# A two-layer streaming encoder step: another order in the attention rounds, a 128-row own block, and tile-by-tile normalisation in the first combine

## The chip, the cores and the metric

The kernel runs on one core of a Trainium2 chip. The metric is the device time of one execution in microseconds (us), as the median of several. The engines named below are TensorE (PE, matrix products), VectorE (DVE), ScalarE (ACT), GpSimd (POOL) and SyncE (SP, which here only issues DMA). They run side by side and meet at semaphores.

## The reference

Two layers run on two groups of tokens with the same weights: 528 prompt tokens (16 learned meta tokens and 512 new ones) and 64 sample tokens, with caches of 512 past tokens for the latter. All is float32, of width 1024.

```
for layer in (0, 1):
    y = even_mixer(x) if layer == 0 else odd_mixer(x)
    x = layer_norm(ALPHA * x + y)
    x = layer_norm(ALPHA * x + moe(x))     # 16 experts, best group of 4, then top 2 in it
```

- The even mixer (layer 0) has four heads of a gated linear recurrence and four heads of forgetting attention ("fox"): softmax(q.k * scale + F_t - F_s) over earlier keys, times v.
- The odd mixer (layer 1) is multi-head latent attention ("MLA") with eight heads: keys and values are made from a 256-wide latent and a rotated 64-wide key shared by the heads. A token sees its own chunk of 64 and all before.
- For a token, the mixture adds the rows of its two experts, each with its weight, to the residual; then comes the normalisation.

## The kernel before, in words

**Tokens and tiles.** The 592 tokens lie in five tiles: tiles 0 to 3 with 128 prompt tokens each, tile 4 with the 64 sample tokens and the 16 meta tokens. The kernel's code is one list of instructions per engine, each in the order of its Python function (`block.tensor`, `block.vector`, `block.scalar`, `block.gpsimd`, `block.sync`). An engine runs its list in order and waits where it says so. PSUM is held as four pairs of banks. Each use of a pair is a ticket; `claim` (PE) waits until the user before it on the pair is released, and `filled` (the reader) waits for PE.

**Attention rounds.** Attention is a list of units, `att_units`. In the fox attention a unit is one head and one tile: four heads of five, 20 units. In MLA the units stand in two groups of four heads; a head has four units for tiles 0 to 3. The sample tokens are computed in the latent space ("absorbed"): one "pair" unit for two heads at a time (128 query rows, 64 own keys and 512 past keys, two sets of value products of 128 latent columns each), after the first and the second head of each group, four in all. One "meta" unit serves the meta tokens of all heads.

A unit goes through these steps, with the line that the profile shows:

- scores: PE multiplies queries with keys (L1330) and adds the mask by a bf16 product with an identity (L1335), in pair 0 or 1 in turn;
- max: VectorE takes the row maximum. In fox it adds the forget sums on the way (L2180) and then negates (L2183); in MLA it is one reduction (L2185);
- exp: ScalarE (L1852 fox, L1859 MLA), with the row sums;
- scale: VectorE inverts the sum (L2191) and scales the row (L2192);
- transposes: PE transposes the own block (L1347) and each block of 128 earlier keys (L1349) into pair 2 or 3 in turn. This claims the pair from the unit two before;
- VectorE copies the own block (L2200), ScalarE the others (L1869);
- values: PE multiplies the own block's values (L1372) and then the others' (L1374) into the same pair;
- output: VectorE copies the result to where the output projection reads it (L2212), which releases the pair.

Rounds interleave the units. In round n, PE does scores of n, values of n-3 and transposes of n-2. VectorE does max of n, output of n-3, own block of n-2 and scale of n-1. ScalarE does exp of n and its copy of n-2. The last unit of a stretch is followed by rounds without scores, the drain. Fox rounds run from 308.8 to 361 us of the span, the MLA groups from 772 to 830 and from 864 to 923.

**The own block.** `own_keys` says which columns of the probabilities are a unit's own keys and at which partitions they land once transposed. For an ordinary unit they are 128 rows, for a pair unit 64 (L1372's weights are then 64 x 128, taken from `cvo`, the latents of tile 4), for the meta unit 16.

**The first combine.** After the experts of layer 0, GpSimd gathers for each token its two experts' rows (L1017). VectorE does for each tile `combine_tile` (L2512, L2514: residual plus two weighted rows), `combined_stats` (L2523 to L2525 statistics, L2529 centring and gain) and `combined_norm` (L2539: scale and offset, into `rb`). Between the last two GpSimd computes the inverse root of the variance in two small operations (L883 adds epsilon, L884 is the power). `combine_tile(1)` stands ahead of `combined_norm(0)`, and so on by one tile. PE waits for the first operation of tile 0's combine, runs 24 products whose result nobody reads (`keep_busy`, L1447), waits for the normalised tile, transposes it (L1105) and begins the next layer's input projection (L1614) as soon as ScalarE has copied the transposes (L1708). The transposes of tile i+1 stand in the midst of tile i's projection.

Of the kernel before, what the change touches and what calls it, by code (L numbers as in the profile page):

```python
# [23 lines left out]
SEQ, NS, NM, PAST = 512, 64, 16, 512  # L24
# [7 lines left out]
QL, KVL, NOPE, ROPE = 512, 256, 128, 64  # L32
# [114 lines left out]
def build_step(nc, const_where, consts, a, o):  # L147
# [11 lines left out]
    with ctx:  # L159
# [116 lines left out]
        cvo = cvb[:, 0, :]  # L276
# [11 lines left out]
        kpst = r2.take(4 * 128).rearrange("p (j n) -> p j n", j=4)  # L288
        qrd = r3.take(4 * 128).rearrange("p (k s) -> p k s", k=4)
        qrm = r3.take(MH * NM)  # L290
        assert max(r2.n, r3.n) <= ARENA - ATT

        rtmp = arena[:, ARENA - 1024:ARENA].rearrange("p (b n) -> p b n", b=4)
# [436 lines left out]
        def own_keys(n):  # L730

            kind, _, i = att_units[n]
            if kind == "pair":
                return slice(NM, 80), slice(0, NS)
            if kind == "meta":
                return slice(NS, 80), slice(NS, 80)
            R = TILES[4] if i == 4 else 128
            return slice(0, R), slice(0, R)
# [360 lines left out]
        def _(pe):  # L1099
# [253 lines left out]
            def att_values(n):  # L1353
# [7 lines left out]
                if kind == "fox":  # L1361
                    hc = slice(128 * h, 128 * h + 128)
                    values = [(fv[rows, 4, hc], [(vp if i == 4 else fv)[:, j, hc] for j in range(nb)])]
                elif kind == "mla":
                    hc = slice(128 * (h % 4), 128 * (h % 4) + 128)
                    values = [(mv_[rows, 4, hc], [mv_[:, j, hc] for j in range(nb)])]
                else:
                    outs.append(psum[pair_of[("PT", n)]][:, 384:512])
                    values = [(cvo[rows, 128 * c:128 * c + 128], [ckpv[:, j, 128 * c:128 * c + 128] for j in range(nb)])
                              for c in range(2)]  # L1370
                for out, (vo, vb) in zip(outs, values):
                    last = pe.matmul(out, vo, pT[rows, n % 2, 512:512 + P], start=True, stop=(nb == 0))  # L1372
# [4 lines left out]
            def attention(first, last):  # L1377
                for n in range(first, last + 3):
                    if n < last:
                        att_scores(n)  # L1380
                    if n - 3 >= first:
                        att_values(n - 3)
                    if first <= n - 2 < last:
                        att_transpose(n - 2)

            pe.wait_ge(*lf_sb["x"])
            pe.wait_ge(*fq_sb[3])
# [56 lines left out]
            def keep_busy(n):  # L1444

                for _ in range(n):
                    pe.matmul(psum[1][:, 0:512], identb[:, :], const("m_past"), start=True, stop=True)  # L1447
# [153 lines left out]
                pe.transpose(ps[:, 768:768 + P], kpb[0:P, i % 2, :], ident[0:P, 0:P]).then_inc(pe_full.sem(("mt", i)), 1)  # L1601

            pe.wait_ge(*cb_sb[(0, "first")])
            keep_busy(24)
            pe.wait_ge(*r_sb[(1, 0)])
            transpose_tile(1, 0, rb[:, 0, :])
            for i in range(NT):
# [407 lines left out]
        def _(dve):  # L2015
# [198 lines left out]
            def attention(first, last):  # L2214
                for n in range(first, last + 3):
                    if n < last:
                        att_max(n)
                    if n - 3 >= first:
                        att_out(n - 3)
                    if first <= n - 2 < last:  # L2220
                        att_own(n - 2)
                    if first <= n - 1 < last:
                        att_scale(n - 1)

            def pad_probs():


                for buf in probs[1:]:
                    dve.memset(buf[:, 0:64], 0.0)
                dve.memset(probs[0][:, 0:64], 0.0).then_inc(pz_sb.sem, 1)  # L2230
# [312 lines left out]
            dve.memset(peT[0:64, 1, :], 0.0).then_inc(pez_sb.sem, 1)  # L2543
            combine_tile(0)
            combined_stats(0)
            combine_tile(1)
            combined_norm(0)
            combined_stats(1)
            combine_tile(2)
            combined_norm(1)  # L2550
            combined_stats(2)
            for i in range(NT):
                if i + 3 < NT:
# [25 lines left out]
            dve.wait_ge(*pe_full[("pt", 3)])  # L2579
            dve.memset(qrd, 0.0)  # L2580
            dve.memset(qrm, 0.0).then_inc(pez_sb.sem, 1)
            pad_probs()
            for g in range(2):
                key = ("qa", g)
# [99 lines left out]
```

## Time and profile before

| what | value |
|---|---|
| median of 3 runs | 1240.25 us (1239.88 to 1240.64) |
| profiled execution, its own time | 1235.15 us |
| its span | 1233.1 us |
| PE busy | 1119.4 us (91%) |
| VectorE busy | 559.4 us (45%) |
| ScalarE busy | 254.0 us (21%) |
| GpSimd busy | 222.4 us (18%) |
| mean granted TensorE clock | 0.97 |

Busy time is the sum of an engine's instructions over the span. Neighbouring products of PE overlap in their records, and their ends are modelled, so the distance between two starts is the better measure of what a product takes. Times in rows count from the start of the span. A bracket at the end of a row gives how long the engine had been idle, and what ended that.

### The profile page before, as it was taken

The numbers are of one execution on the slowest core, as the hardware profiler recorded it, in microseconds if no ns is written. First come the engines' busy times: TensorE is split into PE (matmuls) and PEld (weight loads), VectorE is DVE, ScalarE is ACT, GpSimd is POOL, SyncE is SP. The second block draws the span as 40 slices with busy tenths as digits, with TensorE's granted clock in tenths as the row PEclk, the third lists the DMA queues.
The fourth block names the chain that finished last, engine by engine and source line by source line (L and its number), as shares of the span: only waits on it lengthen the run. The fifth ranks groups of instructions, "written<-read, shape, count | busy, mean of one in ns | idle before, by whom it ended". The sixth has DMA issues, their size and how long they took to land.

```text
span 1233.1 us, 18806 instructions
## 1 busy us (share of the span) xinstructions
PE 1119.4 (91%) x7327; PEld 623.0 (51%) x7332; DVE 559.4 (45%) x1346; ACT 254.0 (21%) x610; POOL 222.4 (18%) x382
## 2 busy tenths in 40 slices
PE   8999999999889979999949989999999988999965
PEld 4556777554664633333315546776774553333312
DVE  2079879610643353744357140440442354554336
ACT  1214245321420000111101122332320000111112
POOL 0106445420201110101044210000000111100114
PEclk9999999999899989999989999999999989999987
DMA  8103302261734186999766222001205175899835
GB/s 355 69 9 141 125 33 105 86 226 65 44 130 175 52 345 246 339 413 375 281 214 222 70 106 69 1 1 68 69 8 231 62 298 209 329 397 407 316 103 196
DMA packets 41974, 215.54 MB, mean 175 GB/s; under 512 B 4504, under 2 KB 6104, under 8 KB 32544
## 3 DMA queue, kind: packets, MB, share of 16 engines
q1 hardware_dynamic: 24432, 153.28, 31.8%
q0 software_dynamic: 17168, 60.27, 15.8%
q8 instruction: 59, 0.97, 0.3%
q10 hardware_dynamic: 288, 0.80, 0.2%
q14 instruction: 27, 0.22, 0.1%
HBM read 181.02 MB, written 33.29 MB: 174 GB/s over the span
## 4 chain that ended last, share of the span: by engine, by line
PE 78%; DVE 9%; issue 4%; DMA 3%; ACT 3%; POOL 1%; DVEq 0%; SPq 0%; ACTq 0%
PE pair L1516 12%; PE pair L1131 9%; PE pair L1410 9%; PE pair L1537 7%; PE pair L1252 5%; PE pair L1330 5%; PE pair L1614 5%; PE pair L1142 4%; PE pair L1374 3%; PE pair L1119 2%; PE pair L1502 2%; PE pair L1372 2%; DMA ring<-in_even_w_in 2%; DMA arena<-x_rows,ints 1%; PE pair L1647 1%
## 5 line engine op out<-in xcount | busy, mean ns | idle before, releaser
L1516 PE MATMUL pair<-ring,arena 128*32 128x512 f32 x608 | 128.5, 595 | 0.0
L1131 PE MATMUL pair<-ring,xT 128*128 128x512 f32 x256 | 111.3, 593 | 0.9 <-DMA ring<-in_even_w_in 0.9
L1516 PE MATMUL pair<-arena 128*32 128x512 f32 x736 | 100.5, 600 | 8.0 <-issue 4.5
L1252 PE MATMUL pair<-xT,ring 128*128 128x296 f32 x320 | 85.1, 421 | 6.9 <-ACT arena L1726 3.0
L883 POOL TENSOR_SCALAR small<-small 128x1 f32<-128x1 f32 (+3 forms) x45 | 15.2, 337 | 386.9 <-DVE small L2264 334.5
L905 POOL TENSOR_TENSOR arena<-arena 128x128 f32<-128x128 f32 x140 | 58.4, 451 | 145.5 <-PE pair L1178 78.9
L1131 PEld LDWEIGHTS pair<-ring,xT 128*128 128x128 f32 x256 | 48.1, 190 | 59.7 <-issue 57.9
L1330 PE MATMUL pair<-arena 128*128 128x264 f32 (+8 forms) x270 | 74.6, 407 | 2.8 <-ACT arena L1716 1.8
L1031 POOL DMA_INDIRECT arena<-x_rows,ints x26 | 26.4, 1014 | 264.9 <-PE pair L1502 163.4
L1252 PEld LDWEIGHTS pair<-xT,ring 128*128 128x128 f32 x320 | 60.4, 193 | 25.8 <-issue 9.3
L2402 DVE COPY arena<-pair 128x256 f32<-128x256 f32 x26 | 11.0, 423 | 135.4 <-PE pair L1525 135.4
L1537 PE MATMUL pair<-ring,arena 128*32 128x512 f32 x304 | 67.5, 611 | 4.0 <-DVE arena L2402 4.0
L1516 PEld LDWEIGHTS pair<-ring,arena 128*32 128x32 f32 x608 | 33.7, 110 | 57.6 <-issue 57.6
L1516 PEld LDWEIGHTS pair<-arena 128*32 128x32 f32 x736 | 30.4, 111 | 63.4 <-issue 63.4
L1614 PE MATMUL pair<-ring,xT 128*128 128x512 f32 (+3 forms) x160 | 57.3, 513 | 1.1 <-ACT xT L1708 1.1
L1410 PE MATMUL pair<-ring,mixT 128*128 128x512 f32 x128 | 57.7, 593 | 0.5 <-issue 0.5
L1410 PE MATMUL pair<-ring,xT 128*128 128x512 f32 x128 | 57.5, 592 | 0.0
L1516 PE MATMUL pair<-xT,arena 128*32 128x512 f32 x320 | 56.3, 592 | 0.0
L1708 ACT COPY xT<-pair 128x1024 f32<-128x1024 f32 (+1 forms) x15 | 14.2, 949 | 189.3 <-PE pair L1105 189.3
L1537 PE MATMUL pair<-arena 128*32 128x512 f32 x368 | 53.1, 608 | 0.0
L1330 PEld LDWEIGHTS pair<-arena 128*128 128x128 f32 (+1 forms) x270 | 43.6, 192 | 12.7 <-issue 5.9
L1374 PE MATMUL pair<-arena 128*128 128x128 f32 (+1 forms) x336 | 48.4, 278 | 0.0
(385 smaller groups left out, 1968.1 us busy)
## 6 DMA issues: line engine op xcount, KB each, us to landing
arena<-in_moe_w_gate_up SPq DMA_DIRECT2D x14, 2048.0 KB, 8.8
ring<-in_moe_w_gate_up SPq DMA_DIRECT2D x12, 2048.0 KB, 9.4
arena<-in_moe_w_down SPq DMA_DIRECT2D x14, 1024.0 KB, 9.2
y_rows<-arena SPq DMA_DIRECT2D x26, 512.0 KB, 8.5
ring<-in_moe_w_down SPq DMA_DIRECT2D x12, 1024.0 KB, 11.3
xT<-in_moe_w_gate_up SPq DMA_DIRECT2D x6, 2048.0 KB, 14.6
ring<-in_even_w_in SPq DMA_DIRECT2D x5, 2048.0 KB, 7.9
y_rows<-xr POOLq DMA_DIRECT2D x12, 512.0 KB, 8.5
```

The source lines that it names most:

```text
L905: last = pool.tensor_tensor(dst, both, mid, ALU.subtract)
L1031: pool.indirect_dma_start(xg[:, e % 2, :], None, x_rows[2 * l], bass.IndirectOffsetOnAxis(ap=sloti[:, e:e + 1], axis=0)).then_inc(xg_in[e ...
L1119: last = pe.matmul(moved(ps, r, lo, n), tokens(c)[:, a:b], w[:, c, m:n], start=(c == 0), stop=(c == K - 1))
L1131: last = pe.matmul(ps[0:P, 0:n], xT[:, k, 128 * i:128 * i + P], w[:, k, :], start=(k == 0), stop=(k == chunks - 1))
L1142: last = pe.matmul(ps[0:w.shape[2], 512 * s:512 * s + n], w[:, k, :], src[:, k, n * s:n * s + n], start=(k == 0), stop=(k == chunks - 1))
L1252: last = pe.matmul(ps[0:w.shape[2], 512 * s:512 * s + n], w[:, k, :], xT[:, k, n * s:n * s + n], start=(k == 0), stop=(k == KD - 1))
L1330: last = pe.matmul(ps[0:P, lo:lo + cols], q_, k_, start=(c == 0), stop=(mask is None and c == len(lq) - 1))
L1374: last = pe.matmul(out, vb[j], pT[:, n % 2, 128 * j:128 * j + P], start=False, stop=(j == nb - 1))
L1410: last = pe.matmul(ps[0:P, 512 * half:512 * half + 512], mixed(k, i), w[:, k, :], start=(k == 0), stop=(k == KD - 1))
L1516: last = pe.matmul(bank[c, :], xgT[:, e % 2, k, c], expert_place(x)[0][:, k, :], start=(k == 0), stop=(k == KD - 1))
L1537: last = pe.matmul(psum[2][c:c + 32, 512 * half:512 * half + 512], hT[:, e % 2, 128 * k + c:128 * k + c + 32], expert_place(x)[1][:, k, 51 ...
L1614: last = pe.matmul(ps[0:P, lo:lo + n], xT[:, k, 128 * i:128 * i + P], w[:, k, :], start=(k == 0), stop=(k == KD - 1))
```

## The change

There are three edits.

1. In the attention rounds PE does the transposes of n-2 ahead of the values of n-3. VectorE does max of n, scale of n-1, own block of n-2, output of n-3, in this order. ScalarE's list is unchanged.
2. A pair unit's own block becomes 128 rows deep: 64 own keys and the first 64 past keys beside them. The values that it meets lie in a new buffer `cvp`, whose upper 64 rows are zero, so that the additional probabilities add nothing.
3. In the first combine each tile is normalised ahead of the next tile's combine, and 17 unread products stand where 24 did.

```diff
@@ regions @@
+        cvp = r3.take(KVL)
@@ own_keys @@
             if kind == "pair":
-                return slice(NM, 80), slice(0, NS)
+                return slice(NM, NM + 128), slice(0, 128)
@@ PE, att_values @@
-                    values = [(cvo[rows, 128 * c:128 * c + 128], [ckpv[:, j, 128 * c:128 * c + 128] for j in range(nb)])
+                    own = cvp if kind == "pair" else cvo
+                    values = [(own[rows, 128 * c:128 * c + 128], [ckpv[:, j, 128 * c:128 * c + 128] for j in range(nb)])
                               for c in range(2)]
@@ PE, attention @@
                     if n < last:
                         att_scores(n)
+                    if first <= n - 2 < last:
+                        att_transpose(n - 2)
                     if n - 3 >= first:
                         att_values(n - 3)
-                    if first <= n - 2 < last:
-                        att_transpose(n - 2)
@@ PE, ahead of the second layer's input projection @@
-            keep_busy(24)
+            keep_busy(17)
@@ VectorE, attention @@
                     if n < last:
                         att_max(n)
+                    if first <= n - 1 < last:
+                        att_scale(n - 1)
+                    if first <= n - 2 < last:
+                        att_own(n - 2)
                     if n - 3 >= first:
                         att_out(n - 3)
-                    if first <= n - 2 < last:
-                        att_own(n - 2)
-                    if first <= n - 1 < last:
-                        att_scale(n - 1)
@@ VectorE, first combine @@
             combine_tile(0)
             combined_stats(0)
+            combined_norm(0)
             combine_tile(1)
-            combined_norm(0)
             combined_stats(1)
+            combined_norm(1)
             combine_tile(2)
-            combined_norm(1)
             combined_stats(2)
@@ VectorE, ahead of the MLA attention @@
             dve.memset(qrm, 0.0).then_inc(pez_sb.sem, 1)
+            dve.memset(cvp[NS:128, :], 0.0)
+            copy(cvp[0:NS, :], cvo[0:NS, :])
```

Tile 3's combine stands in the loop behind, ahead of tile 2's normalisation, as before.

## Rows read from the trace of the kernel before

**Rows 1.** The page's chain that ended last, by engine.

```profile
PE 78%; DVE 9%; issue 4%; DMA 3%; ACT 3%; POOL 1%; DVEq 0%; SPq 0%; ACTq 0%
```

**Rows 2.** PE's waits, 301:361.6, 772:824, 865:923.5: total us, times, longest.

```profile
PE pair L1372 <- ACT arena L1869: 4.9, 9, 1.0
...
PE pair L1372 <- ACT arena L1869: 1.4, 3, 0.5
...
PE pair L1372 <- ACT arena L1869: 3.7, 6, 1.0
```

**Rows 3.** Timeline, fox, one round: start, duration, engine, instruction, [idle before <-releaser].

```profile
329.20 0.38 PE L1335 MATMUL pair<-cstb,identb 80*80 80x512 bf16 x1
...
329.62 0.77 DVE L2180 CUSTOM_DVE_ANT_0 rb<-pair,arena 80x592 f32<-80x592 f32 x1 [0.28 <-PE pair L1335]
...
330.35 0.27 PE L1347 MATMUL pair<-cst,arena 128*128 128x128 f32 x1
...
330.43 0.15 DVE L2183 TENSOR_SCALAR small<-small 80x1 f32<-80x1 f32 x1
...
330.79 0.41 PE L1330 MATMUL pair<-arena 128*128 128x144 f32 x2
...
330.99 0.29 DVE L2200 COPY arena<-pair 128x128 f32<-128x128 f32 x1
...
331.38 0.50 DVE L2192 TENSOR_SCALAR arena<-arena,small 128x528 f32<-128x528 f32 x1
...
331.91 0.49 PE L1372 MATMUL pair<-arena 128*128 128x128 f32 x2 [0.66 <-ACT arena L1869]
```

**Rows 4.** Timeline, drains: first waiting value product (fox), last (MLA, group 0).

```profile
355.15 0.49 PE L1372 MATMUL pair<-arena 128*128 128x128 f32 x2 [0.96 <-ACT arena L1869]
...
828.65 0.49 PE L1372 MATMUL pair<-arena 128*128 128x128 f32 x2 [0.68 <-ACT arena L1869]
```

**Rows 5.** Timeline, MLA: an ordinary value set, then a pair unit's two.

```profile
786.80 0.47 PE L1372 MATMUL pair<-arena 128*128 128x128 f32 x2
...
788.00 0.27 PE L1347 MATMUL pair<-cst,rb 128*64 128x128 f32 x1
...
788.75 0.28 DVE L2200 COPY arena<-pair 64x128 f32<-64x128 f32 x1 [0.25 <-PE pair L1349]
...
789.89 0.19 PE L1335 MATMUL pair<-cstb,identb 128*128 128x64 bf16 x1
...
792.93 0.27 PE L1347 MATMUL pair<-cst,rb 128*128 128x128 f32 x1
```

**Rows 6.** Timelines of VectorE, GpSimd and PE in the first combine.

```profile
640.99 1.28 DVE L2529 SCALAR_TENSOR_TENSOR arena<-arena,small,lng 128x1024 f32<-128x1024 f32 x1
642.19 1.28 DVE L2512 SCALAR_TENSOR_TENSOR arena<-arena,small,xr 128x1024 f32<-128x1024 f32 x1
...
644.70 1.28 DVE L2539 SCALAR_TENSOR_TENSOR rb<-arena,small,lng 128x1024 f32<-128x1024 f32 x1
...
641.05 1.31 POOL L883 TENSOR_SCALAR small<-small 128x1 f32<-128x1 f32 x1 [3.13 <-DVE small L2525]
642.45 1.46 POOL L884 TENSOR_TENSOR small<-small 128x1 f32<-128x1 f32 x1
...
655.39 0.58 POOL L884 TENSOR_TENSOR small<-small 128x1 f32<-128x1 f32 x1
...
638.52 6.27 PE L1447 MATMUL pair<-cstb,identb 128*128 128x512 bf16 x23 [13.25 <-DVE arena L2512]
646.04 1.09 PE L1105 MATMUL pair<-cst,rb 128*128 128x128 f32 x8 [1.25 <-DVE rb L2539]
...
655.21 1.04 PE L1105 MATMUL pair<-cst,rb 128*128 128x128 f32 x8
```

**Rows 7.** PE by window: us, busy (x), granted clock, DMA share, GB/s.

```profile
310.00:312.00 2.00, 1.53 (x3) 0.50 0.22 47
...
645.00:646.00 1.00, 0.00 (x0) 1.00 0.86 247
```

## The prediction

> **What bounds the kernel now.** I read the chain that ended last first: its line by engine is nearly all PE, and everything the change touches lies on that chain [rows 1]. So a step is worth what it takes off TensorE's own sequence. Then I read PE's waits in the three attention stretches: the only large one is a value product (L1372) waiting for ScalarE's copy of the transposed probabilities (L1869), 4.9 us in the forget-gate (fox) attention and 1.4 and 3.7 us in the two windows of latent (MLA) attention [rows 2]. Between those waits PE goes from product to product. The bracketed waits are a little short, because a product's end is modelled some 0.15 us late; I use start-to-start distances below.
>
> Sums are made against the profiled execution (span 1233.1 us, 1235.15 with what lies around it). The median of the timed runs is 1240.25, 5.1 us longer. I take the same difference to hold after, so savings are subtracted from 1240.25.
>
> **1. The new attention order.** A round serves three units: scores of n, transposes of n-2, values of n-3 (before: values, then transposes). The round shown is the one in which the fox scores of the last tile (i = 4, "s4") are n. PE's s4 ends about 329.41 (the mask product starts at 329.20 and streams 512 columns, 0.21 us). Values start 329.58, transposes 330.35 (old order: L1372 first, L1347 after), the next, short scores 330.79 to 331.08, and then the next value product is not released before 331.91: 0.83 us lost [rows 3]. With two smaller losses of 0.17 and 0.33 us in the same head a fox head of 11.62 us loses 1.33 us.
>
> In the new order that wait moves. The transposes of n-2 need the PSUM pair that VectorE's output copy of n-4 frees, and this copy is now last in VectorE's round: max, scale, own block, output. In the s4 round: max from 329.62 to 330.62 (0.77 + read 0.08 + negation 0.15, whose row starts 330.43), reciprocal 0.19, scaling 0.50, own-block copy (next starts 0.21 later), output copy 0.29 [rows 3]. That ends at 331.73, and PE's transposes start at 331.78. PE is there at 329.41 + 0.44 (transposes) + 0.78 (values) + 0.29 (scores) = 330.92, since it no longer waits 0.17 in front of the values. So 0.86 us is lost in place of 0.83: at this place the wait only changes its name, from ScalarE to VectorE. Behind it, however, the values follow the transposes without a wait (ScalarE's copy for them ended 331.86), and so do those of the next rounds. Carried once round the head, the losses are 0.72 (s4 round), 0.04 and 0.13: 0.9 us in place of 1.33, so **0.4 us a head, 1.3 us for three**. The other rounds have scores longer than the 0.55 us that a values-to-output-copy-to-transposes hand-over takes (0.20 to reach VectorE, 0.29 copy, 0.06 back), so they are covered.
>
> The drain at the end of each attention gains more. Fox: each of the last three value products waits, the first up to 355.15 [rows 4]; start to start, with a 0.17 before them, 2.8 us. New: transposes n-2 wait for the s4 round of VectorE, 1.0 us; the last transposes wait 0.55 us for the output copy of the values just made; the last values wait for nothing, since the values before them (1.2 us) cover ScalarE's 0.6 us copy. With 0.13 left before, 1.7 us: **1.1 us saved**. The same walk over an MLA drain (three waits, the last before 828.65 [rows 4], 2.77 us start to start) gives 1.07 + 0.55: **1.15 us saved, twice, 2.3 us**.
>
> Inside MLA the one wait of a head is 0.62 us behind the absorbed unit's scores (four times) and 0.65 us or so behind full scores (twice). VectorE's round gives 0.4 and 0.55 there: 4 x 0.2 + 2 x 0.1 = **1.0 us**.
>
> Sum of part 1: 1.3 + 1.1 + 2.3 + 1.0 = **5.7 us**. Bounds: nothing if each wait only changes its name (0), and all waits gone: 10.0 [rows 2] + 2 (what the brackets miss) = 12. I take 5.7, nearest to the walk.
>
> **2. The deep own block.** An absorbed ("pair") unit's own block has 64 rows as weights; the other products have 128. A normal set of value products (1 own + 4 past) takes 1.20 us from L1372's start 786.80 to L1347's at 788.00. A pair unit has two such sets, and from the mask product at 789.89 to the next transpose at 792.93 it takes 3.04 us; 0.03 + 2 x 1.20 = 2.43 is what two sets of 128 rows would take [rows 5]. The difference, 0.61 us, lies at each change between 64 and 128 rows. Four pair units: **2.4 us**. Bounds: 0 (the gap belongs to something else of these units) to 2.6. All products now have the form of the normal ones, so I take 2.4. Price: a memset and a copy on VectorE ahead of the attention, where it next waits for PE's absorbed queries, and an own block of 128 transposed rows instead of 64, copied by one instruction as before: 0.28 us for 64 rows, 0.29 for 128 [rows 3, 5]. Zero.
>
> The Trainium skill (TensorEngine Tiling (Array Packing), When to Use Tiling) sends a contraction of 64 to 2x row tiling and so speaks against filling up to 128 with zeros; by it the edit would bring nothing or lose. The trace here does not bear it out, as the two halves of the array have no partner product: by that rule the sum would be 2.4 us smaller.
>
> **3. The first combine.** Before, VectorE starts the next tile's combine (642.19, two operations to 644.70) ahead of tile 0's normalisation at 644.70, and PE transposes at 646.04. The normalisation needs VectorE's centring (640.99 + 1.28 = 642.27) and GpSimd's power (L884), which started at 642.45 and took 1.46 us, to 643.91. But L884 took 0.58 at 655.39, between two operations of VectorE [rows 6]. In the new order VectorE is idle from 642.27, so L884 should take 0.58: done 643.03, normalisation at 643.16, 1.54 us ahead. If it stays at 1.46: normalisation at 644.05, 0.65 us. I take **1.5 us**.
>
> The Trainium skill (SBUF — State Buffer, Who interferes with whom) says a VectorE instruction with two SBUF inputs contends with a GpSimd one that reads SBUF. The trace agrees: 1.46 against 0.58 us. Without the rule the sum would be 0.85 us smaller.
>
> The 24 unread products run 638.52 to 644.79 [rows 6]. The seven dropped are the last, at full clock, where 512 columns take 0.21 us: seventeen end at 643.3, ahead of the normalised tile at 644.5, so they don't cost; 24 would have cost 0.3. PE's gap before the transposes stays about 1.2 us. What comes later: tile 1's combine starts 644.4 instead of 642.19, its normalisation ends 651.9 by the same durations (before: 652.5), PE wants it at 653.7 (655.21 less 1.5). Tile 2 and 3 come 1.5 and 0.5 us later than before, but PE wants each over 4 us after it is there. So PE keeps the 1.5 us. GpSimd's gathers for tile 3 move ahead with L884.
>
> Behind each stretch the expert weights are issued by an event of PE's (last values, freed buffers), so they move with it, and nothing there is bound to absolute time. **Sum: 5.7 + 2.4 + 1.5 = 9.6 us, 1240.25 - 9.6 = 1230.7 us.**
>
> **Rivals.**
> - *The new order only renames waits.* For: the s4 round, 0.86 against 0.83 [rows 3]. Against: the drains, where three waits become two. Only parts 2 and 3: 3.9 us, 1236.3. Chance 0.13.
> - *The clock falls in the combine.* About 2 us of idle PE before the fox attention was followed by a half clock at 310 to 312 [rows 7], to about 315. Gaps of 1.2 and 1.1 us stand here too, now behind 1.5 us less of products. Five us at half speed give back 2.5: 1233.2. Against: with the same gaps the clock before stayed at 1.00, as from 645 to 646 with PE idle [rows 7]. Chance 0.1.
> - *The pair unit's gap is not the row count.* 2.4 less: 1233.1. Chance 0.08.
> - *All waits vanish.* Six us more: about 1225. Against: VectorE's round above. Chance 0.07.
> - *VectorE's round binds, slower than before.* If the hand-over isn't covered by the scores, each transposition waits the full round of its own unit: in a fox head VectorE's work is 9.5 us, plus 5 x 0.4 of hand-overs, against PE's 6.5 of transposes and values: 5 us lost a head instead of 1.33, 15 us over four heads, less 3.9: 1251. It decides once the output copy of n-4 ends after the scores of n in most rounds, not in one of five. Chance 0.05.
>
> Main case 0.57, own range 1228.5 to 1233. The range for 8 in 10 takes the renaming case in at one end and goes 3.7 us beyond the sum at the other, over half the way to where all waits vanish: 1227.0 to 1236.5. Faster by over 0.2% (2.5 us, what can be told from no change): 0.91; within: 0.04 (two of the first three rivals together); slower: 0.05.
>
> **What would show it.** PE's waits of L1372 for L1869 nearly gone, and L1347 or L1349 waiting for VectorE's L2212 copy, about 0.7 us once a fox head and 0.4 to 0.6 once an MLA head; L1372 to the next L1347 in pair units 2.4 us; an L884 of about 0.6 us at the start of the combine, and the first transposes 6.0 us after the start of the unread products (before 7.52). The prediction is wrong if the attention stretches from first scores to last values are not 2.4 (fox) and about 2.9 us (each MLA group) shorter.

## The result and the profile after

The changed kernel takes 1227.56 us (1225.18 to 1228.93, 4 runs), the kernel before, run beside it, 1240.07 (1237.09 to 1240.64, 4 runs): ratio 0.9891, 95% interval 0.9865 to 0.9917. That is 12.5 us less by the medians and 10.3 to 16.7 by the interval (1240.07 x 0.0083 and x 0.0135); forecast were 9.6. The direction and the place were right, the size too small by a fifth to a quarter: 1227.56 lies inside the wide range (1227.0 to 1236.5) and below the main case's own (1228.5 to 1233). The profiled execution has a span of 1226.0 us (own time 1227.86).

The page of the changed kernel, busy times and the chain by engine (the chain was [rows 1]):

```profile
PE 1117.2 (91%) x7325; PEld 619.9 (51%) x7325; DVE 558.6 (46%) x1348; ACT 252.3 (21%) x610; POOL 222.4 (18%) x382
...
PE 80%; DVE 9%; issue 4%; DMA 3%; ACT 2%; POOL 1%; DVEq 0%; SPq 0%; ACTq 0%
```

TensorE is still the bound. Its line numbers have moved by one or two: values are L1374 and L1376 (before L1372 and L1374), transposes L1348 and L1350, VectorE's scaling L2194 and output copy L2214.

TensorE's waits in the three attention stretches of the changed kernel (us in total, times, longest); they answer to [rows 2]:

```profile
PE pair L1348 <- DVE xT L2214: 3.3, 5, 0.9
PE pair L1331 <- ACT arena L1718: 1.8, 1, 1.8
PE pair L1348 <- DVE arena L2194: 1.8, 1, 1.8
...
PE pair L1348 <- DVE mixT L2214: 2.6, 5, 1.0
...
PE pair L1348 <- DVE xT L2214: 2.6, 5, 1.0
```

The values' wait for ScalarE's copy is gone from all three lists. The transposes wait for VectorE's output copy instead, five times in each stretch. The two other waits of 1.8 us stand at the start of the fox attention and were there before.

The fox round in which the last tile's scores are n, changed kernel, answering to [rows 3]:

```profile
327.98 0.38 PE L1336 MATMUL pair<-cstb,identb 80*80 80x512 bf16 x1
...
328.39 0.77 DVE L2182 CUSTOM_DVE_ANT_0 rb<-pair,arena 80x592 f32<-80x592 f32 x1 [0.23 <-PE pair L1336]
...
329.21 0.15 DVE L2185 TENSOR_SCALAR small<-small 80x1 f32<-80x1 f32 x1
329.28 0.15 DVE L2193 RECIPROCAL small<-small 128x1 f32<-128x1 f32 x1
...
329.46 0.49 DVE L2194 TENSOR_SCALAR arena<-arena,small 128x528 f32<-128x528 f32 x1
329.88 0.28 DVE L2202 COPY arena<-pair 128x128 f32<-128x128 f32 x1
330.07 0.28 DVE L2214 COPY xT<-pair 128x128 f32<-128x128 f32 x1
...
330.50 0.30 PE L1348 MATMUL pair<-cst,arena 128*128 128x128 f32 x1 [0.59 <-DVE xT L2214]
...
331.08 0.39 PE L1374 MATMUL pair<-arena 128*128 128x128 f32 x2
```

This is the round as predicted: max, scaling, own block, output copy, then the transposes (330.50), and the values behind them without a wait (331.08). The sizes differ: the wait is 0.59 us and not 0.72 to 0.86, and from the max to the end of the copy it is 1.96 us (328.39 to 330.35), not 2.11. The set of values that TensorE makes in between takes 0.67 us (328.77 to 329.44 in the trace); the prediction had given it its old 0.78, and that will matter below.

The first combine of the changed kernel, answering to [rows 6]:

```profile
634.67 6.70 PE L1449 MATMUL pair<-cstb,identb 128*128 128x512 bf16 x17 [12.85 <-DVE arena L2514]
...
637.54 1.28 DVE L2531 SCALAR_TENSOR_TENSOR arena<-arena,small,lng 128x1024 f32<-128x1024 f32 x1
637.60 1.31 POOL L884 TENSOR_SCALAR small<-small 128x1 f32<-128x1 f32 x1 [3.11 <-DVE small L2527]
639.00 0.58 POOL L885 TENSOR_TENSOR small<-small 128x1 f32<-128x1 f32 x1
639.71 1.32 DVE L2541 SCALAR_TENSOR_TENSOR rb<-arena,small,lng 128x1024 f32<-128x1024 f32 x1 [0.89 <-POOL small L885]
...
641.21 1.04 PE L1106 MATMUL pair<-cst,rb 128*128 128x128 f32 x8
```

GpSimd's power takes 0.58 us, not the 1.46 of before. The changed kernel has both cases in itself: 0.58 and 0.57 us for tiles 0 and 1 (639.00 and 646.61), where VectorE is idle, and 1.46 for tile 2 (654.21), where the next combine still runs beside it. From the first unread product to the transposes the rows give 6.54 us for a forecast of 6.0. That is a matter of records: the trace of before holds 23 of the 24 products. The missing one is likely the first, since 638.52 is 0.46 us behind the end of the operation that releases it (L2512, 636.91 + 1.15), against 0.06 us in the changed kernel. The changed kernel's trace has all 17. The distance from the combine's first operation has no such gap: 9.13 us before and 7.75 now.

The rest is read best from stages, each the distance between two starts in a timeline. "Fox" is from the first scores to the output projection, "combine" from its first operation to the first transposes, "latents" from the first query projection (L1647 before) to the first product with the next weights (L1142), "MLA 0" and "MLA 1" from a group's first scores to the product behind its last values. In us:

```
kernel (span)             fox    combine  latents  MLA 0   MLA 1
before, profile (1233.1)  52.83   9.13    22.09    57.72   59.26
before, again   (1238.4)  53.01   9.14    24.74    57.71   59.27
changed         (1226.0)  47.92   7.75    25.93    54.17   55.66
order alone     (1232.1)  49.77   9.23    25.48    55.67   57.15
deep alone      (1231.4)  51.29   9.14    24.82    56.32   57.87
combine alone   (1240.2)  52.96   7.63    25.47    57.71   59.26
```

The MLA stages repeat within 0.02 us from one kernel to another, so terms of 0.1 us can be read there. Fox has two values for the old code, 51.3 and 52.8 to 53.0; the difference is half clock (a granted clock of 0.50) somewhere in 310 to 317 us, which some profiles have and some don't. At full clock, the changed kernel's fox stage is 3.4 us shorter (51.29 less 47.92).

### The profile page after: what moved, and what is told of

It is laid out like the page before. It is cut to its first block, busy times and chain, and to the rows that moved or that the text cites. A ratio compares the mean times of both kernels' runs of the same rounds, so it can differ in the third digit from the quotient of the medians.

```text
span 1226.0 us, 18799 instructions
## 1 busy us (share of the span) xinstructions
PE 1117.2 (91%) x7325; PEld 619.9 (51%) x7325; DVE 558.6 (46%) x1348; ACT 252.3 (21%) x610; POOL 222.4 (18%) x382
## 4 chain that ended last, share of the span: by engine, by line
PE 80%; DVE 9%; issue 4%; DMA 3%; ACT 2%; POOL 1%; DVEq 0%; SPq 0%; ACTq 0%
PE pair L1518 13%; PE pair L1132 9%; PE pair L1412 9%; PE pair L1539 7%; PE pair L1253 6%; PE pair L1331 5%; PE pair L1616 5%; PE pair L1143 4%; PE pair L1376 3%; PE pair L1120 2%; PE pair L1504 2%; DMA ring<-in_even_w_in 2%; PE pair L1649 2%; DMA arena<-x_rows,ints 2%; PE pair L1667 1%
## 5 line engine op out<-in xcount | busy, mean ns | idle before, releaser
L884 POOL TENSOR_SCALAR small<-small 128x1 f32<-128x1 f32 (+3 forms) x45 | 17.7, 393 | 370.8 <-DVE small L2266 322.3
L1132 PEld LDWEIGHTS pair<-ring,xT 128*128 128x128 f32 x256 | 48.1, 190 | 59.8 <-issue 57.9
L1253 PEld LDWEIGHTS pair<-xT,ring 128*128 128x128 f32 x320 | 61.4, 196 | 26.5 <-issue 10.3
L1143 PE MATMUL pair<-arena,ring 128*128 128x296 f32 x192 | 48.4, 413 | 0.0
```

What stands on the lines that cost most here:

```text
L1132: last = pe.matmul(ps[0:P, 0:n], xT[:, k, 128 * i:128 * i + P], w[:, k, :], start=(k == 0), stop=(k == chunks - 1))
L1143: last = pe.matmul(ps[0:w.shape[2], 512 * s:512 * s + n], w[:, k, :], src[:, k, n * s:n * s + n], start=(k == 0), stop=(k == chunks - 1))
L1253: last = pe.matmul(ps[0:w.shape[2], 512 * s:512 * s + n], w[:, k, :], xT[:, k, n * s:n * s + n], start=(k == 0), stop=(k == KD - 1))
```

## Experiments

### One part at a time

**e1_order**, the two orders alone (edit 1), fox and MLA; **e2_deep**, the own block alone (edit 2); **e3_combine**, the combine's order and the 17 products alone (edit 3); **e4_before_again**, no edit, for what a second profile of the kernel before looks like. Their edits are the hunks of the diff above.

> Only the two orders of the attention rounds (TensorE: transposes ahead of values; VectorE: max, scale, own block, output); own block, combine and 24 unread products as before. Theory A (the walk mis-sized the attention, the rest was right): 7 to 9 us faster than before, since the three attention stretches of the changed kernel's trace are shorter by more than the walk gave. Theory B (the walk's 5.7 us is right and what was left out is the clock: the changed kernel's timed runs meet fewer half-clock stretches than those of before): 5 to 6.5 us in the profile's spans of the three stretches at equal clock, and the rest of any difference lies in half-clock slices outside of them. Both: a fox head takes 11.0 us against 11.62.

Measured: 1232.02 us, ratio 0.9922 (0.9903 to 0.9942). Theory A: a fox head takes 11.0 us, and at full clock the three stretches are together 7.4 us shorter (3.2 for fox, less the stall told of below, 2.05 and 2.11), more than theory B's 5 to 6.5.

> Only the pair units' own block is 128 rows deep with zeroed values below; order, combine and unread products as before. Both theories: 2.4 us faster (four times 0.61), from L1372 to the next L1347 in a pair unit 2.4 us instead of 3.0. Rival (the gap is not the row count): same time and 3.0 us.

Measured: 1236.54 us, ratio 0.9970 (0.9955 to 0.9984). The pair units gain 2.8 us together; the rival is out.

> Only the first combine normalises tile by tile, with 17 unread products; attention as before. Prediction's term: 1.5 us faster, with GpSimd's power instruction at 0.6 us. Theory B's rider: with fewer products the half clock may stay longer, which takes up to 1.5 us back, so 0 to 3 us faster.

Measured: 1239.46 us, ratio 0.9986 (0.9972 to 1.0000). The times alone don't tell 1.5 us from nothing; the stage does.

> The kernel before, unchanged, as a kernel of its own. Theory B: its profile shows half-clock slices in other places than the first profile of it did (which had 310 to 315), above all where TensorE waits around 710 and 731 us, and its time differs from the first profiled execution by up to 5 us with them. Theory A: the same slices as the first profile, and ratio 1.000 within 0.002.

Measured: 1241.42 us, ratio 1.0004 (0.9987 to 1.0021). As theory B has it, this profile has half clock at 717 to 721 and 737 to 741 us, where the first had none, and took 1240.92 us to the first one's 1235.15.

The three ratios give 9.7, 3.7 and 1.7 us, together 15; their intervals reach 1.7 to 2.5 us to either side, so they rank the parts and no more. The stages above size them: the order takes 2.05 and 2.11 us off the MLA groups, the deep block 1.40 and 1.39, the combine's edit 1.50 off the combine, and outside fox and latents each leaves the other stages within 0.1 us. The order's fox stage (49.77) holds one stall of 1.7 us that the profile puts down to issue and no other profile shows; without it, 48.1. The changed kernel's MLA groups are 3.55 and 3.60 shorter, 0.1 more than the two parts' sum: here the parts add.

The pair unit with 64 rows (order alone), then with 128 (changed kernel), from the first value product to the next scores:

```profile
792.86 0.48 PE L1372 MATMUL pair<-arena 64*128 64x128 f32 x2
793.27 1.16 PE L1374 MATMUL pair<-arena 128*128 128x128 f32 x8
794.36 0.49 PE L1372 MATMUL pair<-arena 64*128 64x128 f32 x2
794.77 1.16 PE L1374 MATMUL pair<-arena 128*128 128x128 f32 x8
795.77 0.61 PE L1330 MATMUL pair<-arena 128*128 128x264 f32 x2
```

```profile
789.48 0.39 PE L1374 MATMUL pair<-arena 128*128 128x128 f32 x2
789.71 1.06 PE L1376 MATMUL pair<-arena 128*128 128x128 f32 x8
790.60 0.39 PE L1374 MATMUL pair<-arena 128*128 128x128 f32 x2
790.82 1.06 PE L1376 MATMUL pair<-arena 128*128 128x128 f32 x8
791.72 1.06 PE L1331 MATMUL pair<-arena 128*128 128x264 f32 x4
```

2.91 against 2.24 us. From the own block's products to the next start it is 0.41 us with 64 rows and 0.22 with 128, and the eight products behind them take 1.0 to 1.1 us in place of 0.9. So the deep block closes the gap, and the row count is the likely cause. The edit changes the buffer too, and no run parts the two. Few rows alone don't cost it: fox's own blocks of 80 rows take 0.18 us for two products of 80 columns.

### Which half of the order carries it

**e5_pe_order** changes TensorE's order alone:

```diff
                     if n < last:
                         att_scores(n)
-                    if n - 3 >= first:
-                        att_values(n - 3)
                     if first <= n - 2 < last:
                         att_transpose(n - 2)
+                    if n - 3 >= first:
+                        att_values(n - 3)
```

> The kernel before with TensorE's order alone changed (transposes of n-2 ahead of values of n-3); VectorE keeps max, output, own block, scaling. Theory A (the gain sits in TensorE's order: its values no longer wait for ScalarE's copy): the MLA groups (before 57.72 and 59.26 us from first scores to the end of the attention) shorten by 1.5 us or more each and the fox stretch by 2 or more, in all 5 to 8 us, 1232 to 1235. Rival B (VectorE's old order then puts its output copy and the own block between the values and the scaling of n-1, so the next transposes wait some 1 us in short rounds): under half the gain of e1_order is left, 1236 to 1240. Rival C: slower than before, since each round's scaling now waits for the later values; 1242 or more.

Measured: 1247.56 us, ratio 1.0055 (1.0040 to 1.0069): slower than before. Rival C came true. Fox is 56.52 us, the MLA groups 60.95 and 61.61.

**e6_dve_order** changes VectorE's order alone:

```diff
                     if n < last:
                         att_max(n)
-                    if n - 3 >= first:
-                        att_out(n - 3)
-                    if first <= n - 2 < last:
-                        att_own(n - 2)
                     if first <= n - 1 < last:
                         att_scale(n - 1)
+                    if first <= n - 2 < last:
+                        att_own(n - 2)
+                    if n - 3 >= first:
+                        att_out(n - 3)
```

> The kernel before with VectorE's order alone changed (max, scaling of n-1, own block of n-2, output of n-3); TensorE still makes values of n-3 ahead of the transposes of n-2. Theory A: TensorE's waits for ScalarE's copy stay (4.9, 1.4, 3.7 us in the three stretches of before), so nothing is gained: 1239 to 1242, MLA groups within 0.3 us of 57.72 and 59.26. Rival B (earlier scaling is what pays): at least 3 us faster, 1237 or less.

Measured: 1239.76 us, ratio 1.0002 (0.9986 to 1.0019): nothing, as theory A has it. Fox is 51.37 us (no half clock at 310), MLA 57.71 and 59.26.

TensorE's waits in the fox stretch, of e5_pe_order and then of e6_dve_order:

```profile
PE pair L1347 <- DVE rb L2192: 4.6, 6, 1.2
PE pair L1347 <- DVE arena L2192: 4.3, 6, 1.2
```

```profile
PE pair L1372 <- ACT arena L1869: 5.2, 10, 1.0
```

With TensorE's order alone the transposes wait twelve times for VectorE's scaling (L2192), 8.9 us. One of these waits, 0.97 us at the start of the stretch, was there before; the others are 7.9 us in place of the 4.9 for ScalarE: the scaling stands behind the output copy, and that now waits for values which TensorE does last. With VectorE's order alone the old wait for ScalarE stays. By the medians the halves give +7 and about 0 (-1, its interval holds 0), and together -8. TensorE's order removes the wait, and VectorE's is the condition for it.

**e9_vector_dose** does each unit's reciprocal twice, in the changed kernel, which lengthens all rounds of VectorE (57: 20 fox and 37 MLA units; the 28 and 48 in the expectation were miscounted):

```diff
                 chain(dve.reciprocal(rinv[0:P, b:b + 1], rsum[0:P, b:b + 1]))
+                chain(dve.reciprocal(rinv[0:P, b:b + 1], rsum[0:P, b:b + 1]))
```

> The changed kernel with each unit's reciprocal done twice: 0.15 to 0.19 us more in every one of VectorE's rounds (20 fox units and 28 MLA units). Theory A (VectorE's round ends last only where the profile of the changed kernel has TensorE wait for its output copy, five times in each of the three stretches): 15 x 0.19 = 2.8 us at most, 0.6 to 1.1 us in each stretch, 1229 to 1231. Rival B (the round binds everywhere): 48 x 0.19 = 9 us, 1236 or more. Rival C (the hand-over binds, not the round): nothing, 1227 to 1228.

Measured: 1227.95 us, ratio 0.9910 (0.9890 to 0.9931). MLA 0 is 54.98 and MLA 1 56.45 us, 0.81 and 0.79 more than in the changed kernel. Its waits in these two:

```profile
PE pair L1348 <- DVE mixT L2215: 3.4, 5, 1.2
...
PE pair L1348 <- DVE xT L2215: 3.3, 5, 1.2
```

Five waits as before, 0.8 and 0.7 us longer: about 0.16 each, the dose. The other rounds swallow it. The fox stage as a whole (50.51 us) has half clock at 314 to 317 in this profile. Behind that, from the first mask product of a last tile to the output projection, it is 41.70 us against 40.91, again 0.79 more. So the stages say theory A, with 2.4 us in all. The median by itself doesn't: 1227.95 is under A's 1229 to 1231 and within rival C's 1227 to 1228, and only the ratio to the kernel before (0.9910 after 0.9891, intervals overlapping) leans to A. The last rival of the prediction, that VectorE's round binds everywhere, is out either way.

### The unread products

**e7_24_products** is the changed kernel with `keep_busy(24)`.

> The changed kernel with 24 unread products in the first combine instead of 17. Theory: the seven more run at full clock, 0.21 us each, and end 0.3 us or so behind the normalised tile; TensorE reaches the first transposes 0.1 to 0.6 us later: first combine to transposes 7.9 to 8.3 us (7.75 with 17), the whole within 0.6 us of the changed kernel, 1227.5 to 1228.5. Rival (the clock): seven products more keep the clock up behind the combine, 1 to 2 us faster than the changed kernel.

Measured: 1228.54 us, ratio 0.9906 (0.9886 to 0.9926). The combine takes 8.86 us in place of 7.75, so the seven products cost 1.1 us there, and not 0.1 to 0.6. I had timed them at full clock. The rival is out as well, since nothing got faster. TensorE's windows in this combine (us, busy, granted clock, DMA share, GB/s) for the profile of before, and for the changed kernel:

```profile
640.00:641.00 1.00, 1.00 (x5) 0.59 1.03 392
641.00:642.00 1.00, 1.00 (x6) 1.00 1.04 414
```

```profile
639.00:640.00 1.00, 1.00 (x4) 0.50 0.89 146
640.00:641.00 1.00, 1.00 (x5) 0.75 0.93 208
```

The half clock lasted longer here: in the profile of before the full clock came back 2.3 us after the first product on record (638.52), in the changed kernel 5.8 us after (634.67), in e7's own 4.6 us after (634.45). At half clock a product takes 0.43 us, and seventeen of them end just as the tile is ready, at 641.2. Twenty-four stand in its way, by an amount that hangs on when the clock comes back: 1.1 us in e7. With the first profile's clock it would be the 0.3 of the prediction (an estimate: its 24 products ended 7.9 us behind the combine's first operation, and the tile is now normalised at 7.6). So the smaller number belongs to the edit: of the 1.4 us that the combine gains with 17, e7 keeps 0.3 with 24 (9.14 to 8.86).

**e8_fill_latents** follows the half clock further down. The changed kernel's latents take 25.9 us, the first profile of before had 22.1. TensorE's windows there in the changed kernel:

```profile
708.00:710.00 2.00, 1.32 (x6) 0.69 1.02 420
710.00:712.00 2.00, 1.42 (x4) 0.50 1.02 414
712.00:714.00 2.00, 2.00 (x4) 0.50 1.02 430
714.00:716.00 2.00, 2.00 (x4) 0.60 0.34 131
```

In front of them and at their start TensorE idled 1.8, 0.6 and 0.6 us (up to 707.87, 709.05 and 710.58), waiting for ScalarE's copies (L1966). The edit puts unread products into these gaps and into two more around the last tile's latents (0.8 and 1.5 us, at 729 to 732, with half clock behind them):

```diff
+            pe.wait_ge(*ps_free[("mi", 3)])
             for j in range(4):
+                if j >= 1:
+                    keep_busy((0, 7, 2, 2)[j], 0)
                 ps = claim(pe, ("pt", j))
...
                 if i == NT - 1:
+                    pe.wait_ge(*ps_free[("qp", 2)])
+                    keep_busy(3, 0)
                     latents_t(i)
+                    keep_busy(6, 0)
                     rope_t(i - 1)
```

> The changed kernel with 20 more unread products (128 x 512, bf16) in the gaps of TensorE ahead of and among the latent projections: 7, 2 and 2 between the transposes of the past, 3 and 6 around the transposes of the last tile's latents. The profile of the changed kernel has half clock at 708 to 715 and 732 to 735 us behind those gaps, and the stretch from the first query projection to the next weights is 25.9 us; the first profile of the kernel before had no half clock there and 22.1 us. Theory (the 5.1 us between that profile and its median is this clock): with the gaps filled the stretch returns to 22 to 23 us and the time is 2 to 4 us below the changed kernel, 1223.5 to 1226. Rival (the gaps are not what lowers the clock, or the products cost what they save): stretch 25 to 26, time 1227 to 1230.

Measured: 1221.73 us, ratio 0.9852 (0.9830 to 0.9873), so 5.8 us below the changed kernel by the medians and 4.8 by the two ratios to the kernel before: more than the 2 to 4 expected. The latents take 22.09 us, and 2-us windows over the same work read

```profile
704.00:706.00 2.00, 1.74 (x10) 1.00 0.80 264
706.00:708.00 2.00, 1.60 (x9) 1.00 1.02 412
708.00:710.00 2.00, 2.00 (x8) 1.00 1.05 426
```

The stretch is 3.8 us shorter, and the transposes' stage ahead of it 0.7 (5.67 to 5.01); the rest of the medians' difference, 1.3 us, or 0.3 by the ratios, lies within what runs vary. The stretch is 22.08 to 22.10 us in all four kernels with this edit, 24.4 to 25.9 in nine profiles without it, and 22.09 in the first profile of before, which had the gaps but not the half clock behind them. So filling takes away a matter of chance rather than work, and the chance was mostly bad: nine of the ten profiles with the gaps have the half clock.

### Ahead of the fox attention

**e10_fill_fox**, seven unread products more on top of e8, in TensorE's 1.9 us gap ahead of the fox scores:

```diff
             pe.wait_ge(*fkt_sb[4])
+            for _ in range(7):
+                pe.matmul(psum[1][:, 0:512], identb[:, :], const("m_past"), start=True, stop=True)
             pe.wait_ge(*fv_sb[4])
```

> The kernel of e8_fill_latents with seven more unread products in the gap of 1.9 us ahead of the fox scores, where TensorE waits for ScalarE's copies. The profiles of before, e3, e4 and e5 have half clock at 310 to 317 us and a fox stretch 1.6 us longer than e2 and e6; those of the changed kernel and e8 have not. Theory (which of the two happens is a matter of chance, and the gap is what allows it): up to 1.6 us faster in the median than e8, 1220 to 1221.7, no half clock at 310 in the profile. Rival (the changed kernel never has it, so nothing is to be won; seven products of 0.21 us fit the gap): within 0.6 us of e8, 1221.2 to 1222.3.

Measured: 1224.20 us, ratio 0.9884 (0.9862 to 0.9907), so no faster than e8 but 2.5 us slower by the medians, which neither side had expected; the ratios' intervals overlap a little, and the cause of what is more than noise in it is open. Its profile has no half clock at 310, but neither had e8's. The gap is gone, but the stage after it grew from 47.83 to 48.31 us, since the wait of the next experiment grew from 1.7 to 2.2 us. Whether seven products help where the clock would have fallen, the five runs can't tell.

**e11_logf_store_early**, again on top of e8, moves GpSimd's stores of the log-forget rows ahead of those of keys and values:

```diff
+            fp = flf_prompt[0, 0].rearrange("t h -> h t")
+            pool.dma_start(fp[:, NM:NM + SEQ], lf[0:4, PAST:PAST + SEQ], allow_slow_non_contiguous=True).then_inc(lf_st.sem, 16)
...
             def store_rows(i, tile, prompt, sample, sm):
...
                 store_rows(i, fv[:, i, :], v2[0], v2[1], fv_st.sem)
-            pool.wait_ge(*lf_sb["x"])
-            fp = flf_prompt[0, 0].rearrange("t h -> h t")
-            pool.dma_start(fp[:, NM:NM + SEQ], lf[0:4, PAST:PAST + SEQ], allow_slow_non_contiguous=True).then_inc(lf_st.sem, 16)
...
```

> The kernel of e8_fill_latents with GpSimd's store of the log-forget rows (L948 to L950, one of 2.75 us) moved ahead of the key and value stores. In every profile VectorE's first scaling (0.30 us elsewhere) takes 1.7 to 1.8 us and ends when the 2.75 us store issue ends, and TensorE's first transposes wait 1.7 to 1.8 us for it. Theory (the issue on GpSimd holds VectorE): the scaling falls to 0.3 us, the wait to under 0.4, the fox stretch from 47.8 to 46.4 us, 1.2 to 1.5 us faster than e8: 1220.3. Rival (the slow scaling has another cause, such as ScalarE's table load or the first use of the tile): it stays 1.7 us, no gain.

Measured: 1220.06 us, ratio 0.9847 (0.9826 to 0.9869). The first scaling in e8 and then here (L2200 in both; start, duration):

```profile
308.69 2.75 POOL L949 DMA_DIRECT2D out<-arena  x1
309.78 1.69 DVE L2200 TENSOR_SCALAR arena<-arena,small 128x144 f32<-128x144 f32 x1
...
311.44 0.64 POOL L950 DMA_DIRECT2D out<-arena  x1
...
311.52 0.33 PE L1348 MATMUL pair<-cst,arena 128*128 128x128 f32 x1 [1.69 <-DVE arena L2200]
```

```profile
311.51 0.29 DVE L2200 TENSOR_SCALAR arena<-arena,small 128x144 f32<-128x144 f32 x1
...
311.87 0.33 PE L1348 MATMUL pair<-cst,arena 128*128 128x128 f32 x1 [0.30 <-DVE arena L2200]
```

With the store's issue elsewhere the scaling is back to 0.29 us, the wait falls from 1.7 to 0.3, and fox from 47.83 to 46.50 us. The effect and its 1.3 us in the stage are shown; the medians differ by 1.7 us (0.6 by the ratios) with intervals that overlap. The Trainium skill (SBUF — State Buffer, Who interferes with whom) says that a copy or tensor_scalar on VectorE can take the port pair that it shares with GpSimd, and that the later one of the two is then blocked until the other is done. The trace agrees, for a DMA issue as GpSimd's side: 1.69 us, up to the end of the issue, against 0.29 without it. But not every issue holds a scaling: in the changed kernel one of 128 x 272 takes 0.36 us (314.35) beside GpSimd's 0.88 us store issue of 314.22, and also 0.36 in e11 (312.59), where none runs beside it. Why the 2.75 us one does is open.

**e12_all_fills** has the three last edits together.

> e8, e10 and e11 together: the changed kernel with the unread products in both places and the early log-forget store. If the terms add: 1221.7 less 1.4 less 0 to 1.6, so 1218.8 to 1220.4. If the 1.4 us of the scaling was hidden, as e8: 1221 to 1222.

Measured: 1220.05 us, ratio 0.9850 (0.9829 to 0.9872): as e11, within what was expected. It is e11's time with more in it, so the seven products ahead of fox bring nothing here either. Both are faster than the changed kernel and the one before.

## Why the prediction was off

The mechanism held: the value waits for ScalarE (L1869) went, the transposes waited for VectorE's output copy, the pair units' gap closed, the power took 0.58 us. **The step that failed is the walk over the rounds. It gave TensorE's work its old lengths in the new order ("0.44 (transposes) + 0.78 (values)") and put the rounds without a wait at nothing ("so they are covered").** The runs show that the order itself makes TensorE's work shorter. The ordinary value set of [rows 5], which starts at 786.80, in the kernel before:

```profile
786.77 0.19 PE L1335 MATMUL pair<-cstb,identb 128*128 128x64 bf16 x1
...
787.11 1.06 PE L1374 MATMUL pair<-arena 128*128 128x128 f32 x8
```

and the same unit's set in the changed kernel:

```profile
786.13 0.19 PE L1336 MATMUL pair<-cstb,identb 128*128 128x64 bf16 x1
...
786.74 0.39 PE L1374 MATMUL pair<-arena 128*128 128x128 f32 x2
786.96 1.06 PE L1376 MATMUL pair<-arena 128*128 128x128 f32 x8
787.86 1.51 PE L1331 MATMUL pair<-arena 128*128 128x400 f32 x4
```

Before, the set starts right behind the mask product, and its own two products take 0.31 us to the next; now it starts behind the transposes, and they take 0.22. The set is 1.12 us long in place of 1.20. It is so everywhere: in the kernel before, 20 sets with 128 own rows follow a mask product without a wait and take 0.28 to 0.33 us for this step, and the four that follow a score product take 0.22; in e1_order 43 follow transposes, nearly all with 0.22. The first transpose, which now stands behind the mask product, gives back 0.03 us (0.14 to the next in place of 0.11). So rounds in which no wait is marked are mostly 0.05 to 0.1 us shorter. Why a value product behind a mask product takes longer is open.

By terms, the measured sum with the fox stage at full clock is 3.4 + 4.2 + 2.8 + 1.5 = 11.9 us, against 9.6; the interval of the measured difference begins at 10.3.

- **Fox, order: 2.4 forecast, 3.4 measured.** "0.4 us a head, 1.3 us for three" fails. From one head to the next it was 11.62 us and is 11.01 (the mask product of the last tile starts at 327.98 and, in the next head, at 338.99). Of these 0.61 us, 0.40 lie in the two rounds with a marked wait and 0.21 in the three others, in one of which the walk had seen a wait of 0.17 us. The first head adds 0.24 us in its early rounds, which I had not walked, and the drain gave 1.3 for 1.1.
- **MLA, order: 3.3 forecast, 4.2 measured.** The drains are right (2.3, measured 2.3), and so are the waiting rounds: "4 x 0.2 + 2 x 0.1" is 0.5 a group, and from scores to scores these three rounds are 0.22, 0.22 and 0.10 us shorter. What the sum lacks are the other rounds: 0.32 us in group 0 and 0.48 in group 1 (2.67 to 2.62, 2.69 to 2.61 and the like).
- **Deep own block: 2.4 forecast, 2.8 measured**, 0.67 to 0.70 us a pair unit in place of 0.61. The same step again: "2 x 1.20" takes an ordinary set behind a mask product for both. The second set doesn't: in e2_deep the two take 1.19 and 1.12 us. The price was nothing, as forecast.
- **Combine: 1.5 forecast, 1.4 to 1.5 measured.** Normalisation comes 1.54 us earlier, as worked out. "24 would have cost 0.3" holds for the clock of the first profile alone; in e7 it was 1.1.
- **The base.** I took the 5.1 us between the first profile and the median as the same before and after. They are the run's and not the kernel's: the second profile of the kernel before has a span of 1238.4 us and an own time of 1240.9. Of the 5.3 us between the two spans 2.7 lie in the latents, where the first had no half clock; the rest was not taken apart. Subtracting from the median was right even so.

Two slips in the sums did no harm. The terms of VectorE's chain add up to 331.81 and not to 331.73; measured, it is shorter than either, mainly since the reciprocal starts 0.07 us behind the start of the negation (329.21 and 329.28) and the own block's copy 0.42 us behind that of the scaling, not at their ends. And the bound "10.0 + 2" misses the drain of MLA group 0, since the window of [rows 2] ends at 824: over the whole group the waits are 3.7 us and not 1.4.

Of the rivals, "only renames waits" is out by e1_order, the 2.4 us less for a gap that is "not the row count" by e2_deep, and VectorE's round has slack in all but five rounds of an MLA group (e9). "The clock falls in the combine" did not happen in the changed kernel's profile, but it can: e2_deep's has half clock at 645 to 650 us and e5_pe_order's at 651 to 655. What is open is why the half clock near 310 to 317 us came in the profiles of before (twice), e3, e5 and e9 and not in the nine others; it is worth some 1.6 us, and can hold the 0.6 us by which the medians exceed the sum.

## What to carry over

An order of work on two engines that hand over to each other in a ring is one change: the halves alone gave about 0 and +7 us, both together -8. Walk the whole ring, first round and drain included, also the rounds without a wait, since an instruction's length can change with what stands ahead of it. Take the start-to-start distance on the in-order engine, not the durations of its rows. A second profile of the kernel before costs little and tells which stages are the same every time and which depend on the clock that happened to be granted; the gaps in front of those can be worth filling, as they were in the latents (3.8 us of the stage) and were not ahead of fox.

## What was not expected of the hardware

- The granted clock differs between executions of one program: over the 57 runs of the kernel before that stand beside the experiments, the two with a mean clock of 0.964 had a median of 1244.3 us, the fourteen with 0.967 1240.2, the nine with 0.970 1238.0. Gaps of 0.6 to 1.8 us were followed by half clock in some executions and not in others; with the gaps of the latents filled it wasn't seen there in four profiles.
- In the first combine, after 12.8 us or more without products, the full clock came back 2.3 us after the first recorded unread product in one profile and 5.8 in another.
- Two float32 products of 128 x 128 took 0.28 to 0.33 us to the next product behind a bf16 mask product, and 0.22 behind transposes or float32 score products.
- A VectorE scaling of 0.29 us took 1.69 to 1.78 us (2.08 in e10) beside a 2.75 us GpSimd DMA issue (the store of log-forget rows) and ended with it; a 0.88 us issue did not lengthen one of 0.36 us.
- A set of ten products of which the two own ones had 64 rows as weights took 0.33 to 0.35 us longer than one in which all had 128.
